# A decoder block with 32 experts: gate/up weights in 32 KB packets, and x1 stored with its columns regrouped

## What is computed

```python
h = rms_norm(x, attn_norm_w)                      # attention: 8 differential and 8 dilated heads
mix = concat(diff_attention(h), dilated_attention(h))
x1 = x + mix @ w_out
h1 = rms_norm(x1, ffn_norm_w)
logits = h1 @ router_w + router_b                 # 32 experts, the 4 best per token
gates = softmax(top_4(logits))
for each expert e, on the tokens that chose it:
    gu = h1 @ w_gate_up[e] + b_gate_up[e]         # 1024 x 2048
    gate, up = min(gu[:, :1024], 7), clip(gu[:, 1024:], -7, 7)
    act = (up + 1) * gate * sigmoid(1.702 * gate)
    y[token] += gate_of_token * (act @ w_down[e] + b_down[e])     # 1024 x 1024
out = rms_norm(x1 + y, final_norm_w)
```

## Time and profile before

| what | us |
|---|---|
| median of 3 runs | 1086.72 (1086.65 to 1087.52) |
| the profiled execution's own time | 1088.17 |
| its span, first to last instruction | 1086.4 |
| TensorE busy | 1029.8 (95%) |
| TensorE weight loads | 442.3 (41%) |
| VectorE busy | 228.8 (21%) |
| ScalarE busy | 119.5 (11%) |
| DMA, mean over the span | 390 GB/s |

### The profile page before, as it was taken

How to read it: one execution, slowest core, us unless ns; L and a number is a source line. 1 busy time by engine, 2 the same in 40 slices (tenths; PEclk the granted TensorE clock), 3 DMA queues, 4 the chain that set the end, 5 groups by cost and what they waited for, 6 DMA issues and landing times.

```text
span 1086.4 us, 12314 instructions
## 1 busy us (share of the span) xinstructions
PE 1029.8 (95%) x4971; PEld 442.3 (41%) x4971; DVE 228.8 (21%) x508; ACT 119.5 (11%) x287; POOL 10.1 (1%) x25
## 2 busy tenths in 40 slices
PE   7999999999999999989999999899999999999996
PEld 6686554333343432424242424343243434343422
DVE  3566444111111110111111111111111111111111
ACT  1133430000000000000000000000000000000001
POOL 0000000000000000000000000000000000000000
PEclk9999999999999998999999999999999999999999
DMA  9926546999999999999999999999999999999995
GB/s 283 415 103 243 208 171 264 426 429 427 430 428 428 428 428 430 428 429 428 427 431 427 429 428 428 430 427 428 429 427 431 427 428 430 427 431 427 428 428 207
DMA packets 35808, 423.69 MB, mean 390 GB/s; under 512 B 6016, under 2 KB 6032, under 8 KB 11120
## 3 DMA queue, kind: packets, MB, share of 16 engines
q1 hardware_dynamic: 34032, 423.33, 92.7%
q10 hardware_dynamic: 1760, 0.14, 0.1%
HBM read 422.41 MB, written 1.05 MB: 390 GB/s over the span
## 4 chain that ended last, share of the span: by engine, by line
PE 62%; DMA 31%; DVE 4%; ACT 1%; issue 1%; SPq 0%; DVEq 0%; POOLq 0%; POOL 0%; ACTq 0%
PE psum L822 24%; DMA dn_ring<-in_w_down_dram 23%; PE psum L837 17%; DMA gu_ring<-in_w_gate_up_dram 7%; PE psum L567 5%; PE psum L777 5%; PE psum L545 3%; PE psum L664 3%; PE psum L572 2%; DVE shared L1206 1%; DVE shared L1202 1%; DVE shared L1204 1%; PE psum L617 1%; DMA gu_ring<-in_w_in_dram 1%; ACT shared L519 0%
## 5 line engine op out<-in xcount | busy, mean ns | idle before, releaser
L822 PE MATMUL psum<-gu_ring,shared 128*64 128x512 f32 x2048 | 446.8, 593 | 4.7 <-DMA gu_ring<-in_w_gate_up_dram 4.7
L837 PE MATMUL psum<-dn_ring,shared 128*64 128x512 f32 x1024 | 240.1, 620 | 31.7 <-DMA dn_ring<-in_w_down_dram 30.0
L822 PEld LDWEIGHTS psum<-gu_ring,shared 128*64 128x64 f32 x2048 | 143.5, 137 | 287.4 <-issue 275.1
L837 PEld LDWEIGHTS psum<-dn_ring,shared 128*64 128x64 f32 x1024 | 72.9, 142 | 180.4 <-issue 132.2
L1202 DVE TENSOR_SCALAR shared<-psum 128x512 f32<-128x512 f32 x32 | 22.1, 692 | 398.0 <-PE psum L822 398.0
L1151 DVE TENSOR_TENSOR shared<-posm,iota 128x256 f32<-128x256 f32 x47 | 20.0, 425 | 291.1 <-PE psum L545 290.6
L517 ACT ACTIVATE shared<-psum 128x512 f32<-128x512 f32 x32 | 19.1, 597 | 436.7 <-PE psum L822 436.7
L796 PE MATMUL psum<-shared 64*128 64x512 f32 x264 | 65.6, 615 | 0.7 <-ACT shared L510 0.7
L777 PE MATMUL psum<-shared,xres 128*128 128x128 f32 x512 | 63.0, 282 | 1.0 <-DVE shared L1121 1.0
L777 PEld LDWEIGHTS psum<-shared,xres 128*128 128x128 f32 x512 | 61.7, 197 | 1.5 <-DVE shared L1121 1.5
L567 PE MATMUL psum<-gu_ring 128*128 128x256 f32 x256 | 59.3, 390 | 2.1 <-DMA gu_ring<-in_w_in_dram 2.1
(11 more groups left out here) (142 smaller groups left out, 354.0 us busy)
## 6 DMA issues: line engine op xcount, KB each, us to landing
gu_ring<-in_w_gate_up_dram SPq DMA_DIRECT2D x128, 2048.0 KB, 26.4
dn_ring<-in_w_down_dram SPq DMA_DIRECT2D x64, 2048.0 KB, 23.4
gu_ring<-in_w_in_dram SPq DMA_DIRECT2D x11, 1024.0 KB, 18.4
dn_ring<-in_w_out_dram SPq DMA_DIRECT2D x4, 1024.0 KB, 8.9
xres<-in_x_dram SPq DMA_DIRECT2D x2, 512.0 KB, 3.7
gu_ring<-in_w_in_dram SPq DMA_DIRECT2D x2, 512.0 KB, 8.1
out_dram<-hmix SPq DMA_DIRECT2D x4, 256.0 KB, 2.0
dn_ring<-in_b_gate_up_dram SPq DMA_DIRECT2D x3, 256.0 KB, 15.1
```

The lines of the kernel that those rows point to most:

```text
L822: last = mm(bank[2 + b][CAP * c:CAP * (c + 1), :], xg[:, k, CAP * half:CAP * (half + 1)], gu_ring[:, 8 * half + k, w0:w0 + 512], start=Fal ...
L837: last = mm(bank[4][CAP * c:CAP * (c + 1), :], actT[:, a0:a0 + CAP], dn_ring[:, k // 2, w0:w0 + 512], start=False, stop=(k == KT - 1), ski ...
```

## The change

- The columns of x1 are regrouped: within each half of 512 columns, column `4 p + j` is stored at `128 j + p`. VectorE writes it so when it adds, now into `x1`, which lies in the tile `hmix`; `xres` takes ACT's squares in exchange. Turns and gathers then read 128 adjacent columns, and `begin_sum` reads x1 with a step of 128 elements to restore the order.
- Row `512 q + 4 p + j` of the gate/up weights now belongs to step k = 4 q + j. The router's and the norm's weights are loaded in the same order; the logits' scale takes `ffn_p`, and the second parameter load (`ffn_norm_w` in `prm_rows`) is gone.
- For pairs 2 to 12 a half of an expert's gate/up weights is one load of 4 MB with 32 KB per partition, which waits for two quarters to be used, and TensorE waits for the whole half. Pairs 0, 1, 13, 14 and 15 keep loads of 16 KB per partition, now 32 KB apart in memory. The loops on SP and TensorE are divided accordingly (`FIRST` = 2, `LAST` = 3), and the reordering of the last loads begins one pair later.
- `begin_sum(0, 1)` moves behind the first `gate_up`.

```diff
-LAST = 5
+FIRST, LAST = 2, 3
...
+        x1 = hmix
...
-            gu_v = w_gate_up[0, :, :, :].rearrange("e (q p j) c -> p e q (j c)", p=P, j=2)
+            gu_v = w_gate_up[0, :, :, :].rearrange("e (q p j) c -> p e q (j c)", p=P, j=4)
...
-                             gu_v[:, bass.ds(e, 1), q, :]).then_inc(gu_in[s], 16)
+                             gu_v[:, bass.ds(e, 1), q // 2, 2 * WS * (q % 2):2 * WS * (q % 2 + 1)]).then_inc(gu_in[s], 16)
+
+            def load_gu_wide(e, half, h):
+                s = 2 * half + h
+                sp.dma_start(gu_ring[:, 4 * s:4 * s + 4, :].rearrange("p (e j) c -> p e (j c)", e=1),
+                             gu_v[:, bass.ds(e, 1), h, :]).then_inc(gu_wide_in[s], 16)
...
-            with sp.Fori(0, more * PAIRS + (PAIRS - LAST)) as j:
+            def load_gu_half_wide(j, e, half):
+                for h in range(2):
+                    sp.wait_ge(gu_used, j * GUN + (4 * half + 2 * h + 2))
+                    load_gu_wide(e + half, half, h)
+
+            for i in range(FIRST - 1):
+                e = 2 * i + 2
+                load_gu_half(i, e, 0)
+                load_dn_second(i, e - 1)
+                load_gu_half(i, e, 1)
+                load_dn_first(i, e)
+            with sp.Fori(0, more * PAIRS + (PAIRS - FIRST - LAST)) as i:
+                j = i + (FIRST - 1)
                 e = ((j + 1) % PAIRS) * 2
-                load_gu_half(j, e, 0)
+                load_gu_half_wide(j, e, 0)
                 load_dn_second(j, (j % PAIRS) * 2 + 1)
-                load_gu_half(j, e, 1)
+                load_gu_half_wide(j, e, 1)
                 load_dn_first(j, e)
-            for i in range(PAIRS - LAST, PAIRS - 1):
+            for i in range(PAIRS - LAST - 1, PAIRS - 1):
                 j = more * PAIRS + i
                 e = 2 * i + 2
                 for half in range(2):
-                    before = max(0, 3 - (2 * (i - (PAIRS - LAST)) + half))
+                    before = max(0, 3 - (2 * (i - (PAIRS - LAST - 1)) + half))
...
-            act.dma_start(prm_rows[8:16, :], ffn_norm_w.rearrange("o (k p) -> (o k) p", p=P)).then_inc(prm_in, 16)
...
-                    act.dma_start(rw, router_w.rearrange("o (k p) e -> p (o k) e", p=P)).then_inc(rw_in, 16)
-                    act.dma_start(ffn_p[:, :].rearrange("p (q j) -> p q j", j=2),
-                                  ffn_norm_w.rearrange("o (q p j) -> p (o q) j", p=P, j=2)).then_inc(ffn_in, 16)
+                    act.dma_start(rw.rearrange("p (q j) e -> p q (j e)", j=4),
+                                  router_w.rearrange("o (q p j) e -> p (o q) (j e)", p=P, j=4)).then_inc(rw_in, 16)
+                    act.dma_start(ffn_p[:, :].rearrange("p (q j) -> p q j", j=4),
+                                  ffn_norm_w.rearrange("o (q p j) -> p (o q) j", p=P, j=4)).then_inc(ffn_in, 16)
...
-                squares(a).then_inc(sq_done, 1)
+                nc.scalar.activation(xres[:, a, :], x1[:, a, :], ACT.Square, accum_out=st[:, a:a + 1]).then_inc(sq_done, 1)
...
-                turn(bank[b][:, c:c + P], xres[:, a, P * k:P * (k + 1)]).then_inc(x1T_done, 1)
+                turn(bank[b][:, c:c + P], x1[:, a, P * k:P * (k + 1)]).then_inc(x1T_done, 1)
...
-                return mm(bank[(0, 5)[a] + c][:, :], ident[:, :], xres[:, a, 512 * c:512 * (c + 1)], start=True,
+                return mm(bank[(0, 5)[a] + c][:, :], ident[:, :],
+                          x1[:, a, 512 * c:512 * (c + 1)].rearrange("t (j p) -> t p j", j=4), start=True,
                           stop=True, skip_group_check=True)
...
-            begin_sum(0, 0)
-            begin_sum(0, 1).then_inc(bias_used, 1)
+            begin_sum(0, 0).then_inc(bias_used, 1)
...
-                        rows = xres[:, a, :].rearrange("t (q p j) -> t q j p", p=P, j=2)[:, k // 2, k % 2, :]
-                        last = mm(bank[b][:, c:c + P], rows, sel[:, a, :, :].rearrange("p e n -> p (e n)"),
+                        last = mm(bank[b][:, c:c + P], x1[:, a, P * k:P * (k + 1)], sel[:, a, :, :].rearrange("p e n -> p (e n)"),
...
-                    if k % 2 == 0:
-                        pe.wait_ge(gu_in[s], j * 16 + 16)
+                    if narrow and k % 2 == 0:
+                        pe.wait_ge(gu_in[s], 16 * narrow)
+                    elif not narrow and k % 4 == 0:
+                        pe.wait_ge(gu_wide_in[2 * half + k // 4], wide * 16 + 16)
...
-            gate_up(0, 0, first=True)
+            gate_up(0, narrow=1, first=True)
+            begin_sum(0, 1)
             begin_sum(1, 1)
             pe.wait_ge(rounds_ready, 1)
             begin_sum(1, 0)
             more = pe.value_load(more_rounds[0:1, 0:1], min_val=0, max_val=ROUNDS - 1)
-            with pe.Fori(0, more * PAIRS + (PAIRS - 1)) as j:
+            for j in range(FIRST):
                 expert(j, 0)
-                gate_up(j, 1)
+                gate_up(1, narrow=j + 1)
                 expert(j, 1)
-                gate_up(j + 1, 0)
...
+                gate_up(0, narrow=(2, 0)[j])
+            with pe.Fori(0, more * PAIRS + (PAIRS - FIRST - LAST - 1)) as i:
+                expert(i + FIRST, 0)
+                gate_up(1, wide=i)
+                expert(i + FIRST, 1)
+                gate_up(0, wide=i + 1)
+            j = more * PAIRS + (PAIRS - LAST - 1)
+            expert(j, 0)
+            gate_up(1, wide=j - FIRST)
+            expert(j, 1)
+            for i in range(LAST):
+                j = more * PAIRS + (PAIRS - LAST + i)
+                gate_up(0, narrow=FIRST + 1 + i)
+                expert(j, 0)
+                gate_up(1, narrow=FIRST + 1 + i)
+                expert(j, 1, last_one=(i == LAST - 1))
...
             dve.wait_ge(rw_in, 16)
-            V.tensor_tensor(rw, rw, prm[:, 8:16].unsqueeze(2).broadcast_to([P, KT, NE]), ALU.mult).then_inc(rw_ready, 1)
+            dve.wait_ge(ffn_in, 16)
+            V.tensor_tensor(rw, rw, ffn_p[:, :].unsqueeze(2).broadcast_to([P, KT, NE]), ALU.mult).then_inc(rw_ready, 1)
...
-                    xs = xres[:, a, 512 * c:512 * (c + 1)]
-                    V.tensor_tensor(xs, xs, bank[2 * a + c][:, :], ALU.add).then_inc(x1_ready, 1)
+                    apart = "t (p j) -> t p j"
+                    V.tensor_tensor(x1[:, a, 512 * c:512 * (c + 1)].rearrange("t (j p) -> t p j", j=4),
+                                    xres[:, a, 512 * c:512 * (c + 1)].rearrange(apart, j=4),
+                                    bank[2 * a + c][:, :].rearrange(apart, j=4), ALU.add).then_inc(x1_ready, 1)
```

## The result

The changed kernel takes **1090.37 us** in the median of 20 runs (1087.45 to 1092.55), the kernel before 1087.55 in 20 runs beside it (1084.59 to 1089.34). The ratio is 1.0025, with a 95% interval of 1.0018 to 1.0032: 2.8 us slower. Forecast were 1.6 us less. The profiled execution of after took 1091.92 us, with a span of 1090.0.

The account below looks back on a forecast made before the run. The weight stream, from its restart to the last gate/up load, was taken as the bound. Terms -2.8 - 0.3 + 1.1 + 0 + 0.4 + 0 = -1.6 us against the 1086.72 median gave 1085.1 us, range 1082.0 to 1088.6.

Parts of the forecast that it names:

- What bounds the kernel: Weight stream, restart to last gate/up load; the end moves with restart, holes, rate and TensorE catching up at the last load.
- Step 1: Gate/up loads of 22 experts: 352 fewer packets per DMA engine at 7.9 ns fixed cost each, gaining 2.8 us.
- rival (b): Part or all of the fixed cost is per load, or larger: 1079.6 us in full, 1082.3 half-way; chance 0.14.
- rival (c): The rate does not depend on the packet: gain 0, price stays, +1.2 us, 1087.9; chance 0.16.
- Step 3: Hole after expert 0: begin_sum's six strided matmuls before the first down delay w_down; +1.1 us taken, +0.9 to +2.4.
- Rival (d): The six matmuls before down(0): strided moving read at a quarter speed, 1.7 us each, net +7.3, 1094.0 us; chance 0.10.
- Step 2: Stream start: adjacent-column gather saves 0.3 us; strided x1 additions (0 to 0.7) and the dropped parameter load cost 0.
- Step 4: First wide load, waiting for two quarters of expert 2: 0 taken, up to 1 us if it starts more slowly.
- Step 5: TensorE's longer program: 0.165 MB more to bring, costing 0.4 us of the stream, between 0 and 0.8.
- Step 6: Kernel's end, reordered loads a pair later: TensorE just catches up, 0, up to 1.5 us if off.
- Rival (e): The tail: TensorE stays 1.5 us behind at the end, net -0.1, 1086.6 us; chance 0.10.
- Under 1 us: Sign of being right: TensorE's waits for gate/up at the end shrink to under 1 us.

Follow-up runs that it names:

- E1: The changed kernel, but begin_sum reads 512 adjacent columns of x1, leaving the output's x1 part out of order; 1.0011 of the kernel before, 1088.47 us.
- E7: 4 MB gate/up loads made of 16 KB packets, with x1 in the layout of the kernel before; 1.0026 of the kernel before.
- E4: The changed kernel with 32 KB packets but x1 in plain order, begin_sum adjacent and (0, 1) back in its old place; 1.0147, 1102.39 us.
- E3: The changed kernel with all gate/up loads of 2 MB in 16 KB packets; 1.0049 of the kernel before.
- E6: The changed kernel once more, unchanged, for a second trace; 1.0025 of the kernel before.
- E5: The kernel before once more, unchanged, for a second trace; 1.0000 of the kernel before.
- E2: E1 with begin_sum(0, 1) moved back ahead of the counts; 0.9996 of the kernel before.
- E12: The changed kernel with parameter load back, FIRST = 3, ScalarE's plain-order copy of three quarters of x1, first combine left out; 0.9983, 1085.60 us.
- E8: The changed kernel with FIRST = 3, first combine left out, sums moved behind the first down and second gate_up; 1.0020 of the kernel before.
- E9: The changed kernel with the second parameter load of the start put back; 1.0019 of the kernel before.
- E11: The kernel before with ACT's two subln loads held until x has landed; 0.9995 of the kernel before.
- E10: The kernel before with ACT's two subln loads issued ahead of its ffn_norm_w load; 1.0019 of the kernel before.

## Why the prediction was wrong, point by point

**What bounds the kernel: right.** All that moved the end moved the stream: its holes, its rate, its start. One thing is missing from that list: how far apart the 16 parts of the last load land (E1, E7). E4 is the exception, where TensorE became the bound.

**Step 1, packets: right.** 2.8 us were forecast from 4 KB rows; E3 gives 3.3, and the pair of ratios of E3 and E6 (1.0049 and 1.0025, on two chips) 2.6. E7 rules out rival (b), E3 and E7 together rival (c). The 3-cycle overhead in the Trainium skill (DMA: Bandwidth & Descriptors, "Why small descriptors are slow"), an estimated 1.2 us by its clock, does not agree with the 3.3 us that E3 shows.

**Step 3, the hole: the step that failed.** "In proportion to the spacing, 10%, a matmul of 512 takes 0.48 us" is the term that was mis-sized. It measured 0.90, six of them 5.40 us, and the step cost 3.4 us, not 1.1; even the upper bound of 2.4 was too low. The mechanism was right: the w_down issue slipped by as much as the sums grew (22.98 − 19.55 = 3.43), and the DMA engines stood empty in the very microseconds named. The price came from the wrong kind of row, a turn that reads its stationary operand with a step of 16 bytes. It was no guide to a moving operand, and E4 shows that it was none to other stationary reads either: x1 read with that step cost the turns 0.95 us for 0.87, and the gather 7.73 for 3.84. Why turns are spared, no run shows. The next nearest rows, VectorE's strided reduction at 0.7 ns more an element, would have given 0.36 us a matmul on top of 0.46, six of 0.82, or +3.0 for the step. Rival (d) had the right place and direction, with factor two in place of four; its condition, 1.1 us a matmul, was not reached, yet 0.90 us was enough to eat the gain. The cases lacked the middle one.

The rule of the Trainium skill (SBUF — State Buffer, the note on cachelines), which asks for two hits on a line of 16 bytes, agrees with these runs as to which reads pay: 0.90 against 0.46 us a matmul at a step of 512 bytes, and for the gather 3.84 us adjacent, 4.04 with two hits (8 bytes), 7.73 with one (16 bytes). It does not say how much: E4's turns have one hit on a line too, and pay 9%.

**Step 2, start of the stream: half right.** The gather saves 0.20 us (3.84 against 4.04; 0.3 forecast). The two x1 additions cost 0.36 us each (1.05 against 0.69), the upper bound that stood there; about one of them counts in the head of the kernel: from the end of the first 32 projection matmuls to S it is 157.25 us in E5 and 157.31 in E6, with the gather's saving in it. The reason for taking 0, "reading strides, not writing them, is what those rows price", was wrong: writing them costs the same. The first begin_sum took 1.90 us for two matmuls and stayed hidden, as forecast.

**Step 4, first wide load: real, and hidden.** After shows a share of 0.84 at 240 us, E1 0.55, E2 0.63 and 0.53. TensorE and stream were both 3.4 us late after the first hole, so the second had less to take; this reading is argued, not tested. The second hole is half of why E1 gained nothing in L − S, the spread of the parts the other half. With FIRST = 3 it is gone (E12; in E8 no microsecond from 239 to 243 us is under 0.92).

**Step 5, program: right.** The queue of TensorE's program brings 0.33 MB where it brought 0.16; 0.165 more were forecast.

**Step 6, the tail: right.** TensorE waits 2.2 us for gate/up at the end where it waited 4.7, and 2.4 for its last w_down. It still catches up, and end − L is even 0.4 us shorter. Rival (e) is out. "Under 1 us" was too low.

**The start: not foreseen, and only partly shown.** By the cuts, after loses 1.3 us in L − S, gains 0.4 in the tail and loses 0.1 in the head: +1.0. Of the 1.3 in L − S, 3.4 of the hole, 0.4 of program and 0.2 of the dip at 240 us less 3.3 of packets make 0.7, and 0.4 more is that 860 to 1050 us run at 427.1 where they ran at 428.6 GB/s (0.7, less 0.3 of program counted already). The medians say +2.8. The other 1.8 us would have to lie before S, where the forecast held that "The parameter load that goes was one of two small ones beside w_in, for which the start waits: 0." For it: the first 32 projection matmuls end at 18.39, 16.90, 17.74, 18.62 and 18.19 us in the traces of before, E5, E9, E12 and E11, which have the load, 18.0 in the mean; and at 19.56, 18.88, 18.21, 18.32, 18.93, 18.33, 18.76 and 18.68 in after, E6, E1, E2, E3, E4, E7 and E8, which don't, 18.7. For it too: take what each median has above before's and subtract what the kernel's trace has. Without the load 1.7, 1.7, 0.1, 1.9, 1.0, 0.8 and 2.5 us are left (same order, without E4), 1.4 in the mean; with it 0.0, 0.9, 0.1 and −0.6 (E5, E9, E12, E11), 0.1 in the mean. Against it: each of these is uncertain by about 1 us, and E9, the direct test, stands 0.06% below E6, within the noise. A rival was not tested: the clock's fall at the first gather, 1.5 us in the trace of after. It shows in two of the ten traces of changed kernels (after, E4) and in none of the four of before (before, E5, E10, E11); how often it comes among the timed executions, no run shows. So about 1 us by the order of the small loads would fit, and is not settled; the first 32 matmuls take 8.6 to 10.2 us by chance, which hides it in any one trace. It would also cover much of what the medians of E2 and E8 missed.

**The sum** had −1.6 us. With the measured sizes: packets −3.3, head +0.1, hole +3.4, first wide load +0.2, program and the slower end of the stream +0.8, tail −0.4 make +0.8; the start's possible +1 brings it to +1.8, of +2.8 (2.0 to 3.5) measured. Some 1 us stays open.

## What to carry to other kernels

Where a stream of loads bounds a kernel, bytes per packet are worth having, but every microsecond of compute put between the loads' issue and the wait that frees their buffers is paid in full, and relieving one such place may only open the next: cut the trace at the stream's start and at its last load, and count both. Look also at how far apart the parts of a load land, for the last one counts: E1 and E7 each lost over a microsecond that goes with it. Price a strided read on the operation, the operand and the step that it will have: of float32 in matmuls, a step of 512 bytes doubled the time as moving operand, a step of 16 bytes doubled it as stationary operand and one of 8 bytes cost 5%, while turns with a step of 16 bytes lost 9%. If two consumers want two orders, let an idle engine make the second copy.

## What was not expected of the hardware

- A moving operand of 4-byte elements with a step of 512 bytes: 1047 ns a matmul record against 592, 0.90 against 0.46 us in a row of six.
- A stationary one with a step of 16 bytes: 7.73 us for a gather of 32, against 4.04 with 8 and 3.84 with 4. The same read in eight turns: 0.95 us against 0.87.
- VectorE's addition that writes 512 elements with a step of 512 bytes: 1046 against 689 ns.
- A packet's fixed cost of some 9 ns: 3.3 us for 352 packets, the same whether a load has 2 or 4 MB.
- At S + 874 us E1 is 1.3 us of bytes ahead of after, and no earlier at the last gate/up load: its 16 parts land 4.9 us apart, against 3.5 in after and 2.3 in before.
